# A mixture of experts streamed through one core: eight kept weight places instead of six, and the first pair read in row chunks

## The reference

```python
logits = (t @ w_router + b_router)            # 256 tokens, 32 experts
top_logit, top_idx = lax.top_k(logits, 4)
top_w = jax.nn.softmax(top_logit, axis=-1)
# for every expert e, over the tokens routed to it:
gu = xb @ w_gate_up[e] + b_gate_up[e]         # 1024 x 2048
gate, up = jnp.split(gu, 2, axis=-1)
gate = jnp.minimum(gate, 7.0); up = jnp.clip(up, -7.0, 7.0)
act = (up + 1.0) * gate * jax.nn.sigmoid(1.702 * gate)
out = act @ w_down[e] + b_down[e]             # 1024 x 1024
y[token] += top_w * out
```

## Time and profile before

| what | us |
|---|---|
| median of 3 runs | 1299.7 (1297.99 to 1301.95) |
| profiled execution, own time | 1300.82 |
| its span | 1299.0 |
| TensorE busy (matmul) | 1196.8 (92%) |
| VectorE busy | 304.8 (23%) |
| ScalarE busy | 134.9 (10%) |
| DMA, mean over the span | 344 GB/s |

### The profile page before, as it was taken

One profiled execution on the slowest core, in us unless ns is written; L12 is line 12 of the kernel. 1 busy time (PEld: TensorE's weight loads), 2 busy tenths in 40 slices (PEclk: granted clock), 3 DMA queues, 4 the chain that ended last, 5 costly groups with the idle time before them and its releaser, 6 DMA issues.

```text
span 1299.0 us, 14499 instructions
## 1 busy us (share of the span) xinstructions
PE 1196.8 (92%) x5929; PEld 655.9 (50%) x5929; DVE 304.8 (23%) x557; ACT 134.9 (10%) x269; POOL 0.2 (0%) x4
## 2 busy tenths in 40 slices
PE   7999999999998989898989889898989889898988
PEld 6877777888744434242434434242434334242433
DVE  1154322312203213030312213030312213030313
ACT  2233211100201101000000101000000101010001
POOL 0000000000000000000000000000000000000000
PEclk9999999999999999999999999999999999999999
DMA  9622232326666999999999999999999999999995
GB/s 385 269 98 97 98 130 97 121 80 261 252 249 223 430 429 428 428 429 428 428 428 430 428 428 428 428 430 428 429 428 428 428 429 429 428 428 428 429 428 241
DMA packets 35148, 446.29 MB, mean 344 GB/s; under 512 B 3856, under 2 KB 5008, under 8 KB 5424
## 3 DMA queue, kind: packets, MB, share of 16 engines
q1 hardware_dynamic: 34640, 443.63, 81.9%
q10 hardware_dynamic: 480, 2.25, 0.4%
HBM read 444.81 MB, written 1.05 MB: 343 GB/s over the span
## 4 chain that ended last, share of the span: by engine, by line
PE 57%; DMA 38%; DVE 2%; issue 1%; SPq 1%; ACT 0%; DVEq 0%; ACTq 0%
DMA ring<-in_w_down 24%; PE ps L445 20%; PE ps L702 16%; DMA ring<-in_w_gate_up 13%; PE ps L724 11%; PE ps L679 2%; PE ps L745 1%; DMA ring<-in_mix_w 1%; SPq L385 1%; PE ps L711 1%; PE ps L519 1%; PE ps L517 0%; DVE arena L1247 0%; PE ps L499 0%; PE ps L556 0%
## 5 line engine op out<-in xcount | busy, mean ns | idle before, releaser
L702 PE MATMUL ps<-ring,arena 128*64 128x512 f32 x2000 | 464.1, 610 | 44.7 <-DMA ring<-in_w_gate_up 43.3
L702 PEld LDWEIGHTS ps<-ring,arena 128*64 128x64 f32 x2000 | 153.1, 140 | 336.3 <-issue 287.5
L445 PE MATMUL ps<-arena,ring 128*128 128x256 f32 (+1 forms) x1184 | 270.4, 385 | 1.7 <-DVE arena L1131 1.1
L724 PE MATMUL ps<-ring,arena 128*64 128x512 f32 x1024 | 231.2, 604 | 35.0 <-DMA ring<-in_w_down 35.0
L445 PEld LDWEIGHTS ps<-arena,ring 128*128 128x128 f32 x1184 | 222.0, 190 | 41.5 <-issue 8.8
L724 PEld LDWEIGHTS ps<-ring,arena 128*64 128x64 f32 x1024 | 82.5, 139 | 172.4 <-issue 172.4
L1230 DVE COPY arena<-ps 128x1024 f32<-128x1024 f32 x16 | 19.6, 1225 | 473.2 <-PE ps L702 473.2
L967 ACT ACTIVATE arena<-ps 128x1024 f32<-128x1024 f32 x16 | 16.4, 1024 | 618.6 <-PE ps L702 618.6
L1223 DVE TENSOR_TENSOR arena<-ps,arena 128x512 f32<-128x512 f32 x64 | 41.1, 684 | 151.0 <-PE ps L711 151.0
L745 PE MATMUL ps<-arena 128*128 128x256 f32 (+1 forms) x256 | 62.3, 386 | 4.4 <-DVE arena L1247 3.6
L679 PE MATMUL ps<-arena 128*128 128x128 f32 x512 | 62.3, 282 | 1.5 <-DVE arena L1223 1.5
(11 more groups left out here) (179 smaller groups left out, 426.6 us busy)
## 6 DMA issues: line engine op xcount, KB each, us to landing
ring<-in_w_gate_up SPq DMA_DIRECT2D x125, 2048.0 KB, 17.1
ring<-in_w_down SPq DMA_DIRECT2D x62, 2048.0 KB, 17.1
ring<-in_mix_w SPq DMA_DIRECT2D x37, 1024.0 KB, 4.8
arena<-in_w_gate_up SPq DMA_DIRECT2D x3, 2048.0 KB, 10.0
ring<-in_w_down SPq DMA_DIRECT2D x4, 1024.0 KB, 17.9
arena<-in_consts ACTq DMA_DIRECT2D x1, 1424.0 KB, 12.2
arena<-in_xT SPq DMA_DIRECT2D x2, 544.0 KB, 5.2
out<-arena SPq DMA_DIRECT2D x4, 256.0 KB, 2.6
```

Source lines behind the costliest of these rows:

```text
L445: last = mm(ps[:, PROJ + half, 0:rhs.shape[-1]], w[:, k, half * P:(half + 1) * P], rhs, start=(k == 0), stop=(k == KC - 1))
L702: last = mm(ps[half, GATE + b], xeT[:, j, half], w[x][:, at:at + 512], start=(j == 0), stop=(j == 7))
L724: return mm(ps[halves[x], DOWN + b], e_act[:, k, halves[x]], w[:, j * D + b * 512:j * D + (b + 1) * 512], start=(k == 0), stop=(k == 7))
```

## The change

The six double places and two of the spare ones become one ring of eight that is kept for good (`homes`); `spare[1]` is used once, as before. Transfer number t of the stream, counted from unit 0 of the first pair on, without the one in `spare[1]`, goes to home t % 8. Twelve units per pair and eight places repeat every two pairs, so the loops of SP and TensorE take two pairs per turn (`odd` says which of the two), with one or two pairs written out before them and the last after them. `last_m` is now computed on each engine from `over_i`, which is 0 here.

In the first pair each place holds row chunk j of both experts (two runs of 8 KB per partition) instead of two row chunks of one expert, and a place is counted free after each chunk (`gate_up_both`). The first two places of the second pair do the same. The gather of pair 1 moves to before the last row chunk of the first gate-up; it goes to the banks DOWN and on, and its columns to `xeT_1`. The transposes of pair 0 go to DOWN and ADD too. The second gate-up follows them at once, without a wait for `gate_read` or `up_biased`, and the bias add-back of pair 0 comes behind it.

```diff
+        xeT_1 = cut(r_gate, 0, (KC, 2 * CAP))
...
-        def first_place(q):
-            if q in (3, 4):
-                return spare[q - 3], spare_landed[q - 3], 16
-            d = {0: 1, 1: 2, 2: 3, 5: 4, 6: 5, 7: 0}[q]
-            return double(d), pair_landed[d], 16
-        def place(m, q):
-            if isinstance(m, int) and m == 0 and q == 0:
-                return spare[2], spare_landed[2], 16
-            return double(q % DOUBLES), pair_landed[q % DOUBLES], 32 * m + 16 * ((q + 5) // DOUBLES + 1)
+        homes = ((double(1), pair_landed[1]), (double(2), pair_landed[2]), (double(3), pair_landed[3]),
+                 (spare[0], spare_landed[0]), (double(4), pair_landed[4]), (double(5), pair_landed[5]),
+                 (double(0), pair_landed[0]), (spare[2], spare_landed[2]))
+        def first_place(j):
+            if j == 4:
+                return spare[1], spare_landed[1], 16
+            dst, arrived = homes[j if j < 4 else j - 1]
+            return dst, arrived, 16
+        def place(m, q, odd=None):
+            if isinstance(m, int):
+                turn_no = 12 * m + q + 7
+                dst, arrived = homes[turn_no % 8]
+                return dst, arrived, 16 * (turn_no // 8 + 1)
+            turn_no = 12 * odd + q + 7
+            dst, arrived = homes[turn_no % 8]
+            return dst, arrived, 24 * (m - odd) + 16 * (turn_no // 8 + 1)
...
+            def both_experts_source(lap, j):
+                i, jj = divmod(j, 2)
+                return w_gate_up[2 * lap:2 * lap + 2].rearrange("o (i p j) n -> p i j o n", i=4, j=2)[:, i, jj]
             def slot_free(m, q):
-                if q >= 6:
-                    sp.wait_ge(gu_used, 8 * m + q + 3)
-                elif q < 2:
-                    sp.wait_ge(gu_used, 8 * m + q + 7)
+                if q >= 8:
+                    sp.wait_ge(gu_used, 8 * m + q + 1)
+                elif q < 4:
+                    sp.wait_ge(gu_used, 8 * m + q + 5)
                 else:
-                    sp.wait_ge(dn_used, 4 * m + q - 5)
+                    sp.wait_ge(dn_used, 4 * m + q - 7)
...
             def second_units():
                 for q in range(12):
                     if q == 0:
                         sp.wait_ge(u2_turned, 2)
-                    elif q < 4:
+                    elif q < 5:
                         sp.wait_ge(gu_used, q)
-                    elif q < 7:
-                        sp.wait_ge(gu_used, q + 2)
+                    elif q < 8:
+                        sp.wait_ge(gu_used, q + 1)
                     else:
                         slot_free(0, q)
...
-            with sp.Fori(1, last_m + 1) as m:
-                lap = sp.compute_val((m + 1) & 15)
-                before = sp.compute_val(m & 15)
-                pair_units(m, lap, before)
+            pair_units(1, 1, 2, 1)
...
+            with sp.Fori(2, last_m, 2) as m:
...
+                pair_units(m, 0, lap_1, lap_0)
+                pair_units(m + 1, 1, lap_2, lap_1)
+            pair_units(last_m, 0, 15, 14)
...
+            def gate_up_both(j, home, columns):
+                w = landed_unit(home)
+                for b in range(4):
+                    for x, half in enumerate(halves):
+                        at = x * 2048 + b * 512
+                        last = mm(ps[half, GATE + b], columns[:, j, half], w[:, at:at + 512], start=(j == 0), stop=(j == 7))
+                last.then_inc(gu_used, 1)
...
             def first_pair():
-                gate_up(0, first_place)
-                turn_hidden(0)
+                pe.wait_ge(xe_ready, 1)
+                for j in range(7):
+                    gate_up_both(j, first_place(j), xeT)
                 pe.wait_ge(sel_ready, 2)
-                pe.wait_ge(gate_read, 1)
-                gather()
+                gather(DOWN)
+                gate_up_both(7, first_place(7), xeT)
+                pe.wait_ge(xe_ready, 2)
+                turn_hidden(0, DOWN)
+            def second_gate_up():
+                for j in range(2):
+                    gate_up_both(j, place(0, j), xeT_1)
+                for i in range(1, 4):
+                    gate_up(i, lambda q: place(0, q), xeT_1)
+                pe.wait_ge(up_biased, 1)
                 pe.wait_ge(bdown_in, 16)
                 add_back(0, b_dn, wgtT)
...
-            hidden(0, 0)
-            columns_read(1)
+            columns_read(1, xeT_1, DOWN)
+            hidden(0, 0, DOWN)
             add_up(0)
```

More of the change, by code:

```diff
@@ L687, in landed_unit, with gate_up, turn_hidden @@
                 return dst
[L689 to L707, removed]
+            def gate_up_both(j, home, columns):
[5 more added lines that the diff above has]
+                last.then_inc(gu_used, 1)
+            def gate_up(i, where, columns):
+                w = [landed_unit(where(2 * i + x)) for x in range(2)]
+                for jj in range(2):
+                    j = 2 * i + jj
+                    for b in range(4):
+                        at = jj * 2048 + b * 512
+                        for x, half in enumerate(halves):
+                            last = mm(ps[half, GATE + b], columns[:, j, half], w[x][:, at:at + 512],
+                                      start=(j == 0), stop=(j == 7))
+                            if jj == 1 and b == 3:
+                                last.then_inc(gu_used, 1)
+            def turn_hidden(n, bank):
                 pe.wait_ge(raw_copied, 2 * n + 2)
                 for c in range(16):
-                    last = turn(ps[:, GATE + c // 4, (c % 4) * P:(c % 4 + 1) * P], gu_raw[:, c], ident)
+                    last = turn(ps[:, bank + c // 4, (c % 4) * P:(c % 4 + 1) * P], gu_raw[:, c], ident)
                 last.then_inc(gu_turned, 1)
@@ L748, in first_pair, with pair @@
             def first_pair():
-                gate_up(0, first_place)
-                turn_hidden(0)
+                pe.wait_ge(xe_ready, 1)
+                for j in range(7):
+                    gate_up_both(j, first_place(j), xeT)
                 pe.wait_ge(sel_ready, 2)
-                pe.wait_ge(gate_read, 1)
-                gather()
+                gather(DOWN)
[8 more added lines that the diff above has]
+                pe.wait_ge(up_biased, 1)
                 pe.wait_ge(bdown_in, 16)
                 add_back(0, b_dn, wgtT)
-            def pair(m, last_pair):
-                gate_up(m + 1, lambda q: place(m, q))
+            def pair(m, odd=None, last_pair=False):
+                if not (isinstance(m, int) and m == 0):
+                    pe.wait_ge(xe_ready, m + 2)
+                    pe.wait_ge(up_biased, m + 1)
+                    for i in range(4):
+                        gate_up(i, lambda q: place(m, q, odd), xeT)
                 pe.wait_ge(act_ready, m + 1)
@@ L764, in pair @@
                     pe.wait_ge(eout_ready, 2 * m)
-                down(0, [landed_unit(place(m, 8 + x)) for x in range(2)])
-                turn_hidden(m + 1)
-                down(1, [landed_unit(place(m, 10 + x)) for x in range(2)])
+                down(0, [landed_unit(place(m, 8 + x, odd)) for x in range(2)])
+                turn_hidden(m + 1, GATE)
+                down(1, [landed_unit(place(m, 10 + x, odd)) for x in range(2)])
                 turn_weighted(m)
@@ L784, in _ @@
             pe.wait_ge(bias_ready, 1)
-            gather()
+            gather(GATE)
             pe.wait_ge(wgtT_ready, 1)
             first_pair()
+            second_gate_up()
             pe.wait_ge(pairs_ready, 1)
[L790 to L794, removed]
+            over = pe.value_load(over_i[0:1, :], min_val=0, max_val=48)
+            last_m = pe.compute_val(over + 14)
+            pair(0)
+            pair(1)
+            with pe.Fori(2, last_m, 2) as m:
+                pair(m, 0)
+                pair(m + 1, 1)
+            pair(last_m, 0, True)
             pe.wait_ge(act_ready, last_m + 2)
             pe.wait_ge(eout_ready, 2 * last_m + 2)
-            down(0, [landed_unit(place(last_m + 1, x)) for x in range(2)])
+            down(0, [landed_unit(place(last_m + 1, x, 1)) for x in range(2)])
             turn_weighted(last_m + 1)
-            w = (double(2), double(3))
+            w = [place(last_m + 1, q, 1)[0] for q in (2, 3)]
             for h in range(2):
```

66 lines of the change are left out of this document (38 added, 28 removed).

## The result

| | before | after |
|---|---|---|
| median, us | 1299.86 (4 runs) | 1284.41 (4 runs, 1282.37 to 1285.82) |
| ratio to before | 1 | 0.9882, 95% interval 0.9863 to 0.9901 |
| profiled execution, own time / span, us | 1300.82 / 1299.0 | 1283.94 / 1281.4 |

The change makes the kernel 15.5 us faster by the medians; 1282.1 was forecast, 1277 to 1292 the range. Both intervals hold 13 to 14.8 us; I take 14 as the change's worth.

The account below looks back on a forecast made before the run. The prediction took the expert stage as bound by one full weight-transfer stream, with gain only in its early holes. Span 1299.0 - 17.6 = 1281.4, own time 1283.2, less 1.1 for the median gives 1282.1 us; range 1277 to 1292.

Parts of the forecast that it names:

- What bounds: Expert stage: one stream of 192 transfers of 2 MB limits, 58.7 us a lap; only holes before 422 us can be won.
- Row chunks, first issues: First gate-up: TensorE frees one place each 3.46 us, so SP issues at 365.6, 369.1, 372.6 and 376.0.
- slow-chunk rival: First pair's row chunks arrive slowly: above 9.9 us a chunk the kernel is slower, 1321 at 12 us; chance 0.06.
- Early gather: Second pair's gather, 3.81 us, moved before the first gate-up's last chunk; second gate-up starts at 396.9 instead of 403.34.
- Clock in the second gate-up: Second gate-up's first quarter takes the normal 6.9 us instead of 8.8; if the clock falls all the same, 1.9 us lost.
- Ring of eight: Earlier issues land the second group's last unit at 423.3 against 441.2, next pair's unit 11 at 482.4 against 500.0: 17.6 us.
- The rule: Weight stream: a transfer lands at the later of its issue + 7.6 us and the previous landing + 4.89 us.
- A full stream can't gain from a deeper ring: nothing.: Later laps: a ring of eight frees places two units sooner than six, but the full stream gains nothing.
- TensorE is what is late next, around 460: Second pair: unit 8 is 0.4 us late; further TensorE loss before 460 us goes into the stream one to one.
- Size of the runs: Row chunks in 8 KB runs: full speed assumed, from a 431 GB/s load at the start; other end twice the time.
- No gain: Whole kernel: the holes are worth nothing because TensorE limits just behind, time stays at 1299.7; chance 0.07.
- The head start is lost on TensorE's side: Second gate-up starts only near 403.3 instead of 396.9: a gain of 10 us, time 1290; chance 0.12.

Follow-up runs that it names:

- e1: The change with its ring of eight only: whole units and the second pair gathered after the first gate-up, as in the kernel before; ratio to before 0.9969.
- e2: The full change without row chunks (ring of eight and early gather, all transfers whole units in 16 KB runs); ratio to the kernel before 0.9904.
- e3: The full change without the early gather (ring of eight and row chunks, second pair gathered after the first gate-up); ratio to the kernel before 0.9933.
- e11: The full change, unaltered, timed again beside other kernels; ratio to the kernel before 0.9905, median 1287.75 us.
- e5: The full change plus 64 unused matmuls on TensorE, once, between the second gate-up and the bias add-back; ratio to the kernel before 0.9946.
- e6: The full change plus one extra gather (3.6 us of TensorE) in each of the loop's 12 pairs; ratio to the kernel before 0.9885.
- e7: The full change with all 192 units, gate-up and down, as row chunks of both experts in 8 KB runs; ratio to the kernel before 0.9945.
- e9: The full change with only the down units of the last two pairs (8 units) as row chunks of both experts; ratio to the kernel before 0.9867.
- e10: The full change, but from the third pair on gate-up units are read in 8 KB runs, one expert per transfer; ratio to the kernel before 0.9951.

## Why the prediction was right

- **What bounds.** Right: the stream from 442 on is as full and as fast as before, a lap 58.7 us, and the gain lies in the holes before 422.
- **Row chunks, first issues.** Right: issues at 363.06, 366.49 and so on, 3.4 us apart. All are 2.5 us earlier than written (365.6, 369.1), most of it by the clock of that run (the gather took 3.57 us, before 6.01). One reading was incomplete: the first unit of the first pair goes out at 277.02 us, not at 290.84, which I took for the first of eight; it changes nothing but the price of the slow-chunk rival.
- **Early gather.** Right: 3.77 us moved, one wait of 1.42 us (1.2 forecast), second gate-up 3.3 us behind the first. From e1 to e2 it brings 8.5 us, where the forecasts differ by 8.1; from e3 to the change 3.6 to 6.6, where 7 was forecast.
- **Clock in the second gate-up.** Right, it stayed at full speed. That the clock before the first gate-up and in the first down would differ from run to run I didn't see; it cost 2.6 and 1.4 us in e11's profile, so a pair of profiles can be 4 us off.
- **Ring of eight.** The step's size was too large. The rule (issue + 7.6, previous + 4.89) leaves out that the stream, once refilled, doesn't hold 428 GB/s: after the change it moved 434 from 366 to 390 us, but 385 from 391 to 403 and 358 from 408 to 414, at a DMA share of 0.99 and 0.95. These two are worth 2.2 us, of which the rule has 1.1 (it waits for the issues of units 8 and 10). By L - S the rule misses 1.4 us more after the change than before, 2.7 in e11. Why the rate falls there, the runs don't show.

```profile
391.00:403.00 12.00, 10.60 (x58) 4.74 (x60) 7.55 (x9) 3.37 (x3) 0.00 (x0) 1.00 0.99 385
408.00:414.00 6.00, 6.00 (x30) 2.01 (x28) 0.00 (x0) 0.00 (x0) 0.00 (x0) 1.00 0.95 358
```

- **"A full stream can't gain from a deeper ring: nothing."** Nearly: in most profiles it loses. In the change's the last lap's landing is 1.2 us late (1216.70 + 30.44, which is 59.9 us after 1158.19 + 29.04), in e1 and e11 by 0.9 and 1.6. But in e5, with the same eight places, it comes 58.7 us after the one ahead, so eight places alone don't bring it about. The cause is open; the transfer was issued 30 us ahead, in time.

```profile
1163.75 28.60 DMA ring<-in_w_down
...
1221.82 29.27 DMA ring<-in_w_down
```

- **TensorE is what is late next, around 460.** Right, by e5; that from the third pair on it isn't, by e6.
- **Size of the runs.** Full speed was 1.4% too good, read from a load at the start that lasts a few us. In the change no cost shows (e2, without them, isn't faster); nine of ten chunks are issued by 345.58, ahead of the hole. Kept for the whole stream it would eat most of the gain (e7).
- **The sum.** 17.6 us: less 1.4 to 2.7 for the refilled stream and 0 to 2 behind L is 13 to 16; the two timings of the change give 12.3 and 15.3. That the first pair of spans differ by exactly 17.6 is luck: 2.7 us of clock and start stand against what the sum had too large. e11's median, 1287.75, lies in the stated range, but above the main case's own (1279 to 1286).
- **Rivals.** "No gain" and "slower" are out. "The head start is lost on TensorE's side" (1290) is what e3 builds, and it measures 1292; the change itself doesn't lose it. The row-pitch rule of the Trainium skill (DMA: Bandwidth & Descriptors, Latency and other measured facts), 103 GB/s at 8 MiB between the rows of neighbouring partitions, would have made a chunk some 20 us long (an estimate), had it held between the two halves of one partition. With two experts 8 MiB apart in each gate-up transfer a unit of e7 takes 4.97 us (2.1 MB at 422 GB/s), so the rule doesn't reach this layout.

## What to carry to other kernels

When a transfer stream is full for most of the span, look for its holes and for who frees the places then; a landing table made by hand from issue times, with one latency and one time per transfer, priced the change and four partial versions of it in their right order, to within 3 us of their first timings. An engine with spare time on average can still be the one that is late for a while after the start: what it does there costs most of what it lasts (e5), later the same work is free (e6). Two timings of one kernel can lie 3 us apart by the clock that its executions were granted, so look at it before a small gain is believed. Fine-grained units pay where a wait is near (the tail, by e9; the start, by e1 to e3, though with the early gather in place nothing of it showed) and cost where the stream is full, so use them near waits alone.

## What the runs showed of the hardware that was not expected

- Transfers of 2 MB in runs of 8 KB ran at 422 GB/s against 428 for runs of 16 KB, at the same DMA share of 1.01 (e7). With one expert per transfer and two thirds of the units in such runs it was 424 (e10).
- With all transfers in runs of 8 KB and eight places, SP's issue instruction itself took 4.5 us in the median and up to 8.6, where it takes 0.33 else (columns: shortest, median, longest in ns; e7 first, then the change). In e10, with two thirds of the units in such runs, the median stayed at 0.37. e7's DMA share was 1.01 all the same, so the engines didn't run dry.

```profile
L401 SPq DMA_DIRECT2D ring<-in_w_gate_up x40: 372/4478/8574, 600.5 to 999.1; - x40
```

```profile
L401 SPq DMA_DIRECT2D ring<-in_w_gate_up x41: 332/333/333, 607.3 to 999.4; - x41
```

- The granted clock from 352 to 362 us was 1.00 in one run and 0.66 in another of the same kernel, behind the same wait of 1.68 us; it made the gather 2.6 us longer.
